# Moving the stationary tiles of two products and of the input projection to other addresses modulo 512 bytes

## The reference, cut to what matters

```python
h_in = rms_norm(x, pre_mix_norm_w)                       # x: 1 x 2048 x 1024, float32
proj = h_in @ w_in                                       # 1024 -> q, k, v, o, gates, value, gate
qk   = silu(causal_depthwise_conv(qk_raw, width 4))
y_m  = sigmoid(o) * group_norm(mlstm_chunkwise(q, k, v, i, f)) * w   # 4 heads x 128, chunks of 128
u    = causal_depthwise_conv(val * sigmoid(gate), width 31)
y_c  = silu(group_norm(u) * w + b)
x    = x + rms_norm(concat(y_m, y_c) @ w_out, post_mix_norm_w)
h2   = rms_norm(x, pre_mlp_norm_w)
a    = relu(h2 @ w_ff1)                                  # 1024 -> 4096: "the first product"
x    = x + rms_norm((a * a) @ w_ff2, post_mlp_norm_w)    # 4096 -> 1024: "the second product"
```

## Time and profile before

| | us |
|---|---|
| median of 2 runs | 2107.64 |
| lowest, highest | 2107.47, 2107.82 |
| span of the profiled execution | 2109.4 |
| phase A's and B's matmuls, to the last of L1332 | about 861 |
| first product (L1861) | about 862 to 1490 |
| second product (L2079) | 1490 to 2103 |

### The profile page before, as it was taken

The page is one execution under the profiler, slowest core; times in us unless marked ns, Lnnn a source line. Parts: engine busy times, 40 slices in busy tenths (PEclk is TensorE's granted clock), DMA queues, the critical chain, the costliest instruction groups (busy, mean ns, idle before and its releaser), DMA issues. The chain is left out here.

```text
span 2109.4 us, 26456 instructions
## 1 busy us (share of the span) xinstructions
PE 2065.3 (98%) x9843; PEld 1719.6 (82%) x9843; DVE 1441.5 (68%) x1979; ACT 913.2 (43%) x1545; POOL 414.6 (20%) x252
## 2 busy tenths in 40 slices
PE   7999999999999999899999999999999999999998
PEld 4897878878788888688888788888788888888887
DVE  5797999989567777876667866666663536534286
ACT  5633334343445444655445644554432313313163
POOL 0000000000001322333322322332262144400012
PEclk9999999999999999999999999999999999999999
DMA  5031212113656865854455655445766455443376
GB/s 201 11 101 51 70 40 77 54 30 107 195 165 205 264 225 167 269 175 136 153 164 179 235 165 157 138 145 172 254 227 249 163 206 187 167 167 137 140 250 219
DMA packets 253118, 338.53 MB, mean 160 GB/s; under 512 B 11584, under 2 KB 193600, under 8 KB 239168
## 3 DMA queue, kind: packets, MB, share of 16 engines
q1 hardware_dynamic: 220352, 315.80, 44.9%
q10 hardware_dynamic: 32384, 20.98, 3.1%
q0 software_dynamic: 256, 0.07, 0.0%
HBM read 225.58 MB, written 111.21 MB: 160 GB/s over the span
## 5 line engine op out<-in xcount | busy, mean ns | idle before, releaser
L1861 PE MATMUL psum<-x_hi,w_hi_P 128*128 128x512 f32 x896 | 350.5, 391 | 12.3 <-DVE x_lo L1805 6.2
L2079 PE MATMUL psum<-w_hi,hid_hi 128*128 128x512 f32 x896 | 349.3, 390 | 2.0 <-DVE hid_lo L1957 2.0
L1861 PE MATMUL psum<-x_lo,w_hi_P 128*128 128x512 f32 x896 | 349.6, 390 | 0.0
L1861 PE MATMUL psum<-x_hi,w_lo_P 128*128 128x512 f32 x896 | 349.5, 390 | 0.0
L2079 PE MATMUL psum<-w_lo,hid_hi 128*128 128x512 f32 x896 | 349.3, 390 | 0.0
L2079 PE MATMUL psum<-w_hi,hid_lo 128*128 128x512 f32 x896 | 349.1, 390 | 0.0
L1957 DVE TENSOR_TENSOR hid_lo<-hid_raw,hid_hi 128x1024 fp32r<-128x1024 f32 x112 | 176.7, 1615 | 207.4 <-ACT hid_hi L1952 207.3
L1774 POOL TENSOR_TENSOR w_raw<-w_raw 128x512 f32<-128x512 f32 x128 | 181.5, 1439 | 410.7 <-DVE w_lo_P L1787 388.5
L1952 ACT ACTIVATE hid_hi<-hid_raw 128x1024 fp32r<-128x1024 f32 x112 | 113.0, 1051 | 342.6 <-DMA hid_raw<-scratch_hid 342.6
L1787 DVE TENSOR_TENSOR w_lo_P<-w_raw,w_hi_P 128x512 fp32r<-128x512 f32 x224 | 184.6, 836 | 107.2 <-ACT w_hi_P L1783 104.2
L1783 ACT ACTIVATE w_hi_P<-w_raw 128x512 fp32r<-128x512 f32 x224 | 136.8, 627 | 255.7 <-PE psum L1861 249.3
(11 more groups left out here) (280 smaller groups left out, 3762.0 us busy)
## 6 DMA issues: line engine op xcount, KB each, us to landing
scratch_hid<-stage SPq DMA_DIRECT2D x224, 256.0 KB, 3.6
hid_raw<-scratch_hid SPq DMA_DIRECT2D x56, 1024.0 KB, 4.9
w_raw<-in_w SPq DMA_DIRECT2D x52, 1024.0 KB, 5.0
w_grain<-in_w SPq DMA_DIRECT2D x48, 512.0 KB, 5.0
x_raw<-scratch_h2s SPq DMA_DIRECT2D x14, 1024.0 KB, 8.5
w_raw<-in_w_in SPq DMA_DIRECT2D x22, 512.0 KB, 3.6
scratch_h2s<-h2s SPq DMA_DIRECT2D x8, 1280.0 KB, 9.2
scratch_qk<-qout ACTq DMA_DIRECT2D x16, 512.0 KB, 3.0
```

The source lines that it names most:

```text
L1861: mm = nc.tensor.matmul(psum[:, bank_1(op, g), :], l, r, start=kt == 0 and i == 0, stop=kt == 3 and i == 2)
L2079: mm = nc.tensor.matmul(psum[:, bank, :], l, r, start=f == 0 and k == 0, stop=f == NFP - 1 and k == 2)
```

## The change

`w_hi` starts 256 bytes later: the pad ahead of it grows from 120 to 184 words, and the pad of 64 words behind it goes, so that `w_lo` and all that follows stay where they are. Slot 7 of the first product's moving tiles is moved by 320 bytes. The three slots of `hid_hi` and `hid_lo` move by 384, 256 and 128 bytes, and accumulators 0 to 9 by 256 bytes to make room. No instruction, no wait and no transfer is added or taken away.

```diff
-PAD_A, PAD_W, PAD_B = 120, 64, 24
+PAD_A, PAD_W, PAD_B = 184, 0, 24
@@ phase_a
         w_hi_all = sb("w_hi", [P, w_cols], F32R)
         gates = keep["gates"] = sb("gates_c", [P, 2, H, NCH])
-        sb("pad_w", [P, PAD_W])
@@ phase_c
-    x_at = [203.5, 0, 32, 16, 48, 105, 121, 167]
+    x_at = [203.5, 0, 32, 16, 48, 105, 121, 167 + 5 / 16]
@@
-    hid_at = [121, 48, 105]
+    hid_at = [121 + 3 / 8, 48 + 1 / 4, 105 + 1 / 8]
@@
-    acc = [at(f"acc{t}", 64 + 4 * t if t < 10 else 97.5 + 4 * t, (D,)) for t in range(S // P)]
+    acc = [at(f"acc{t}", 64 + 1 / 4 + 4 * t if t < 10 else 97.5 + 4 * t, (D,)) for t in range(S // P)]
```

## The result

| | before | after |
|---|---|---|
| median of the runs, us | 2107.64 (2 runs) | 2120.25 (2 runs: 2119.57, 2120.93) |
| after / before | | 1.0052, 95% interval 1.0036 to 1.0068 |
| span of the profiled execution, us | 2109.4 | 2119.1 |
| first to last matmul, us | 2093.1 | 2104.5 |

The change makes the kernel slower, by 0.5%: the ratio gives 11.0 us (7.6 to 14.3), the two medians differ by 12.6, where 22.4 were forecast. A second comparison on one chip (further down) gives 1.0054, 1.0041 to 1.0066.

A forecast was written before the change was run, and what follows sets the result against it. The prediction took the spacing of matmuls on PE as the bound: 4064 matmuls x 5.5 ns = 22.4 us, all else 0, so 2107.6 + 22.4 = 2130.0 us, with 2090 to 2158 us as the range for 8 in 10.

The forecast's parts named there:

- The mechanism: On PE, weight loads beside the moving stream cost some 20 to 50 cycles; equal-address trains settle at 226.7 ns.
- ScalarE, VectorE, the transfers and the accumulators at 0: Outside PE's matmul spacing: moved tiles, transfers and accumulators were each forecast to cost 0 us.
- The price of 5.5 ns: Per 512 wide matmul with changed distance: +5.5 ns, the middle of +4.3 and +6.7, giving 22.4 us.
- ten unsettled intervals: Output projection after a wait: first ten intervals average 231.0 ns, +4.3 ns, taken as the nearest row for lost cadence.
- one step of 6.67 ns: Spacing of 512 wide matmuls one step up: 233.3 ns, +6.7 ns over the settled 226.7.
- the count: 512 wide matmuls with changed distance: 2688 second product, 192 first product, 1024 and 160 projection, sum 4064.
- The 264 column run of the earlier trace: Projection's 264 wide matmuls, at unequal distances: 10.8 ns over their columns instead of 13.3, used as the lower bound.
- The count in the projection: Two of three matmuls have w_hi in them: 1024 of L423's 1536 and 160 of L404's 240.
- The cadence stays: Rival, all stretches: every matmul keeps 226.7 ns, no change, 2107.6 us; chance 0.22.
- The new distance is better: Rival, 512 wide matmuls: 2.5 ns cheaper each, 2097 us, or one step down, 2080 us; chance 0.17.
- The -2.5 ns of the earlier trace: Projection's 264 wide matmuls: 10.8 against 13.3 ns over columns, taken as the lower bound of the price per matmul.
- Two steps up: Rival, 512 wide matmuls: each weight load collides fully, 240.0 ns, 54 us, 2162 us; chance 0.19.

The follow-up runs named there:

- h128: Against before, only the second product's three stationary slots moved, all by 128 bytes (and accumulators 0 to 9); ratio 1.0063 (1.0047 to 1.0079), 13.3 us slower.
- map1: Computation left out, 59 bare trains of 48 float32r matmuls, each at one fixed distance between stationary and moving tile; 226.7 ns at distance 256, 233.3 at 128.
- w128: Against before, only the projection's w_hi moved, by 128 bytes instead of the change's 256; ratio 1.004 (1.0025 to 1.0054), 8.4 us.
- map2: Computation left out, 48 bare trains with alternating distances, fewer stationary columns, 256 columns or bfloat16; bfloat16 215.7 ns, alternating patterns 229.9 to 234.8 ns.
- best: Against before, projection weights of v's second pair and of o put at distance 192, three tile loads waiting for one more ring slot; ratio 1.0021 (1.0011 to 1.0032).
- map3: Computation left out, 42 bare trains: widths 128 to 512, repeated distances, one odd matmul in three; distance 0 and 256 at 226.7 ns, 192 at 228.9, then 233.3.

## Why the prediction went as it did

The mechanism was right as far as it went: PE's spacing is all that the change touches, a train of equal addresses keeps a good cadence, a train at another distance can lose it, and nothing else moves. ScalarE, VectorE, the transfers and the accumulators at 0 were right, within 1 us.

The price of 5.5 ns came out: 5.8 ns in slots 0 and 2, 5.7 in h128. That it came so near is in part luck. It was the middle between the mean of ten unsettled intervals at equal addresses and one step of 6.67 ns, the same for every distance, while in map1 the price runs from 2.1 ns (distance 192) to 7.7 (96) with the distance; both lossy slots happen to lie at 128. For slot 7, at 192, it was 3.6.

The step that failed is the count. The prediction multiplied by 4064, all 512 wide matmuls whose distance changed by anything modulo 512, and gave no reason why a move by 256 should cost as much as one by 128. The period is 256 bytes, so slot 1's steps (19 of 56) and the projection's 1184 matmuls keep their cadence. What loses it is 37 steps of 48, 1776 matmuls, and slot 7's 192: 1776 x 5.8 = 10.3 us, 0.6 us for slot 1's steps, which settle anew after each change of slot (227.3 ns), and 1.5 us around slot 7, 12.4 us in all, against 22.4. The trace of before couldn't have told this. The 264 column run of the earlier trace rows passes distance 256 at kt 0, but with three matmuls at each distance nothing settles: by kt its intervals are 119.1 ns at kt 0, 119.0 at kt 3 and up to 123.3 at kt 7. It took the trace of after, or bare trains.

The count in the projection would have been off in the other way had the distance been 128: two of three matmuls were counted, and w128 shows that all three pay.

The rivals. *The cadence stays* was half right: it holds for every move by 256 and for no other part. *The new distance is better* is refuted at 512 columns: of all distances in the map none is under 226.7. The -2.5 ns of the earlier trace rows came from another width, and widths don't compare: at 256 columns other distances are cheaper than 0, with 113.3 to 118.7 ns at most of them in map2 against 120.0. The change left that alone only because it moved these matmuls' w_hi by 256. *Two steps up*, 240 ns, is the mean of no train; it occurs in single intervals, up to 241 ns at distance 128 and one in four where 0 and 32 alternate.

The rules of the Trainium skill. "TensorE: Matmul & The Clock Gate", section "Back-to-back issue gap", has an isolated gap of 215.8 ns for 512 columns: the bfloat16 trains, which are streams and not isolated matmuls, stand at 215.7. The float32r trains, at 226.7 in the best case, don't agree. "SBUF — State Buffer", section "Who interferes with whom", has TensorE's two read ports independent and TensorE never waiting: in bfloat16 the trains agree, in float32r they disagree by 2 to 8 ns a matmul over the settled ones, by distance alone.

What would show it was put as 1710 to 1745 matmuls in the window of 400 us, and perhaps an alternation between slots: 1735 it is, and slot 1 stands out.

## What to carry to other kernels

Where TensorE is the bound, the operands are float32r and the matmuls 512 columns wide, put the stationary and the moving tiles of a train at the same address modulo 256 bytes; a tile that lies 128 off costs 2.5% of its matmuls' time, and costs its neighbours in the train some of theirs. Do not carry this to other widths unmeasured: at 256 columns the equal address is not the cheapest, 120.0 ns against 117.8 and 113.3 at distance 192 in the kernel. Read it from the spacing of the matmuls' starts, by step or slot, since the busy share (98% in both kernels) and the waits don't show it. When an effect may be periodic in an address, find the period with bare trains before counting what it touches. And look at the intervals one by one before a mean is believed: in best the mean said that nothing was gained where each matmul was faster.

## What the runs showed of the hardware that was not expected

- The period of 256 bytes, and that the good distances reach 16 bytes to either side (240 and 16: 226.7 ns) while 32 bytes already cost 6.7 ns.
- Off the good distance the spacing has several values for the same distance (192: 228.8 or 233.3 ns; 256 columns at 64: 113.3 or 117.8 ns). Which of them comes isn't explained by these runs; at 512 columns only the settled one, at distance 0, came out the same every time.
- Fewer stationary columns do not bring a float32r matmul of 512 columns under 226.7 ns: at distance 0 it takes 230.0 ns with 64 and 231.7 with 32, where 128 take 226.7. At distance 128 they are cheaper than 128 columns: 229.3 and 230.8 against 232.2 to 233.5.
- A float32r matmul of 128 columns took as long as 512 columns are wide, 213.3 ns at all four distances, where 192 columns took 111.6 to 111.8 at three of the four (at distance 0 the train fell from 213 to 111 on its way). The row of a 128 column train of map3:

```profile
35.81 6.82 PE L56 MATMUL psum<-mv,st 128*128 128x128 f32 x31
```

- In best the granted clock stood at 0.50 from 516.3 to 519.7 us, behind a wait of 3.06 us and 1.4 us of matmuls, and 256 column matmuls started 213 ns apart instead of 113 to 118. Whether the wait brought it about wasn't tested.
- What in the chip gives the 32 cycles and the 256 bytes stays open: that float32r has them and bfloat16 has not is all that was shown; no other type was tried.
